# First mixer reworked: transposed input, norm after the projections, decay sums spread by transfers, memory projections a unit later

## The chip, the cores and the metric

The kernel runs on one core of one Trainium2 chip. The metric is the device time of one execution in microseconds (us); of several runs the median is given. The engines are named as in the profile: PE is TensorE's matmul, PEld its weight load, DVE is VectorE, ACT is ScalarE, POOL is GpSimd, SP is SyncE, whose queue issues every large transfer of this kernel.

## What is computed

A decoder trunk of two layers over 256 tokens of width 1024, in float32. Layer 0 mixes with a Mamba-2 scan (SSD), layer 1 with windowed attention; each also attends to 256 memory tokens and ends in a mixture of 32 experts. The parts of the reference that the change touches:

```
proj = rms_norm(h, norm_w) @ in_w
z, xbc, dt, q_mem = jnp.split(proj, [...], axis=-1)
xbc = jax.nn.silu(causal_depthwise_conv(xbc, conv_w, conv_b))
dt = jax.nn.softplus(dt + dt_bias)
# scan over 2 chunks of 128 tokens, 4 groups of 6 heads:
acum = jnp.cumsum(ac, axis=1)
seg = acum[:, :, None] - acum[:, None, :]
decay = jnp.exp(jnp.where(causal, seg, -jnp.inf))
y_diag = jnp.einsum('blsgr,bsgrp->blgrp', cb[..., None] * decay, xc)
...
kv = (rms_norm(mem, norm_w) @ w_kv)       # memory attention, in each layer
```

## The kernel before, in words

The program is a row of stages: the first mixer (`mixer_a`, 0 to about 289 us), the experts of layer 0 (to about 760 us), the second mixer, the experts of layer 1, the final norm.

**First mixer.** PE, DVE and ACT walk the same list, `order`, of small units of work such as `("conv", 3)` or `("yd", 0)`; each engine does its part of a unit and waits on semaphores for the others. A unit owns a PSUM bank, handed out in list order by `Units`. The list goes: `xT`, four units that turn the normed input by PE transposes (L336), behind the norm, which ACT and DVE do first on rows (L415 to L425); `dt`, 16 small matmuls whose stationary operand is the turned input (L893); 20 `conv` units, the projection of 128 channels each as 8 matmuls of 128x256 (L397), of which DVE makes the convolution (L1034, L1036) and ACT the silu; six `z` units (matmuls of 128x512) with transposes between; and then the scan. The scan has eight steps (2 chunks by 4 groups). Step i has `("cb", i)`; two `A` units, in which PE spreads the running sum of one head over all partitions, by a matmul of the broadcast `adt` column with the triangle (L930, 6 matmuls in a step); the decay arithmetic on DVE and ACT in four buffers `E` (L1060, L807, L988); and `("yd", i)`, the product with them (L956), one step later. A list `between` puts projections for the memory attention into each step. Then come `outm` (L365) and `out` (L380), the output projection, and the router.

**Transfers.** Weights pass through 18 slots of 1 MB (`own`, `late`, `extra`). SP issues the loads in the order of use, each when the slot's last user has finished, so one wait holds back everything behind it. The layer's first 18 expert loads follow the mixer's.

**Experts.** Twelve units a layer (`units_of`): eight wide ones with two experts of 64 tokens (12 loads of 1 MB each), four narrow ones with four experts of 32 tokens (24 loads each). A unit: gate and up projections (L1407), gather for the next unit (L1382), down projection (L1416), scatter (L1399). At the head of the units in `SIDE`, in layer 0 alone, PE also makes one of the two memory projections for layer 1 (`side`, L1438 and L1441); their weights are two 1 MB loads each, put in front of that unit's. Before the router's counting matmuls, PE does three idle matmuls (L513).

Of the kernel before, what the change touches and what calls it, by code (L numbers as in the profile page):

```python
# [28 lines left out]
P = 128  # L29
# [18 lines left out]
NEG = -1e30  # L48
GRAN = 2048
# [9 lines left out]
FIELDS = [("ident", P), ("tri", P), ("ones", P), ("iota", SEQ), ("band_prev", P), ("band_cur", P),  # L59
          ("index8", EG), ("cos", NT * 16), ("sin", NT * 16),  # L60
          ("a_norm", KD), ("mem_norm0", KD), ("mem_norm1", KD), ("kv_norm", KD), ("b_norm", KD),
          ("ffn_norm0", KD), ("ffn_norm1", KD), ("ffn_rows0", KD), ("ffn_rows1", KD), ("conv_w", NCONV * 4), ("conv_b", NCONV), ("gnorm", INNER // P),
          ("dt_bias", SSD_HEADS), ("a_log", SSD_HEADS), ("d_skip", SSD_HEADS), ("sinks", Q_HEADS),
          ("route_b0", NG + NE), ("route_b1", NG + NE), ("route_w0", KD * (NG + NE)), ("route_w1", KD * (NG + NE)),
          ("dt_w", KD * SSD_HEADS)]
# [20 lines left out]
SIDE = [NU - 4, NU - 2]  # L86
# [355 lines left out]
class Router:  # L442
# [51 lines left out]
    def pe(self, pe, key):  # L494
# [123 lines left out]
def mixer_a(c):  # L618
# [5 lines left out]
             "out_tile mem1_dve " + Router.SEMS)  # L624
    s = c.sems("mixer", names)
    ld_small = c.sem("ld_small")
    ld_x, ld_mem = ([c.sem(f"ld_{n}{t}") for t in range(NT)] for n in ("x", "mem"))
    with ctx:
# [13 lines left out]
        cbm = [sb(f"cbm{i}", P) for i in range(2)]  # L642
        xw = [acc[:, i * GW:(i + 1) * GW] for i in range(2)]
        sq = xw

# [13 lines left out]
        order = [("xT", i) for i in range(4)] + [("dt", 0)]  # L659
        order += [("conv", j) for j in range(NCONV)]  # L660
        order += [("z", 0), ("xtok", 0), ("xtok", 1), ("xtok", 2), ("bt", 0), ("ac", 0), ("z", 1), ("xtok", 3), ("xtok", 4), ("xtok", 5)]
# [14 lines left out]

        def freed(kind, i):
# [4 lines left out]
            return {"xT": (s["xT_ev"], 2 * i + 2), "dt": (s["dt_dve"], 1), "conv": (s["conv_dve"], 4 * i + 4),  # L682
                    "xtok": (s["xtok_ev"], i + 1), "bt": (s["bt_ev"], 1), "ac": (s["ac_dve"], 2), "z": (s["z_ev"], i + 1),
                    "q": (s["q_ev"], i + 1), "memT": (s["mem1_dve"], i + 1), "mk": (s["mk_ev"], i + 1),
                    "mv": (s["mv_ev"], i + 1), "cb": (s["cb_dve"], i + 1), "A": (s["seg_dve"], 3 * i + 3),
# [5 lines left out]
        U = Units(c, order, freed, holds)  # L691
# [18 lines left out]
        x_norm = Norm(c, c.h, 0, s["x_act"], s["x_dve"])  # L710
# [7 lines left out]
        def _(sp):  # L718
            for t in range(NT):
                sp.dma_start(cut(c.h, t=NT)[:, t, :], g["x"][0, t * P:(t + 1) * P, :]).then_inc(ld_x[t], 16)  # L720
            sp.dma_start(c.small[:, :], g["small"]).then_inc(ld_small, 16)
            for n in range(2):
                c.load_mixer_tile(sp, n)
# [1257 lines left out]
```

## Time and profile before

| | |
|---|---|
| median of 3 runs | 1394.44 us (1393.88 to 1397.04) |
| the profiled execution, its own time | 1395.1 us |
| its span, first to last instruction | 1393.2 us |
| PE busy | 1243.3 us, 89% |
| DVE, ACT busy | 280.8 us, 205.9 us |
| DMA, mean over the span | 329 GB/s; 427 GB/s where it is full |
| mean granted clock | 0.956 |

The span in 40 slices gives each about 34.8 us: the first mixer is slices 1 to 8, the experts of layer 0 slices 9 to 22. A busy PE in such a table is not a PE at its peak. Each matmul in float32 shows as two records in the trace, so "x16" is eight matmuls.

### The profile page before, as it was taken

What the parts mean: (1) busy time and instruction counts of PE and PEld (TensorE: products, weight loads), DVE (VectorE), ACT (ScalarE), POOL (GpSimd) and SP (SyncE); (2) the same over time, 40 slices, a digit from 0 to 9 for tenths busy, and PEclk for the clock granted to TensorE, in tenths of its full rate; (3) what the DMA queues carried; (4) which work ended last, traced back from release to release, by engine and by line L of the source; (5) the groups of instructions that cost most, each with busy time, mean ns of one, the idle gap of its engine ahead of it and who ended that gap; (6) DMA issues with size and microseconds to landing.
All of it is one profiled execution on the core that took longest, in us unless ns stands there. A gap on an engine that the chain in (4) does not pass through costs nothing. (4 is left out here: it accounts for less than half of the span.)

```text
span 1393.2 us, 15227 instructions
## 1 busy us (share of the span) xinstructions
PE 1243.3 (89%) x6130; PEld 627.0 (45%) x6130; DVE 280.8 (20%) x679; ACT 205.9 (15%) x490; POOL 34.0 (2%) x42
## 2 busy tenths in 40 slices
PE   6999999989999999769686998999999999757685
PEld 6875876454444445313232566454444443322221
DVE  3542453041111110100002156031111111100001
ACT  3124233120000000000002246130000000000001
POOL 0001210000000000000000011000000000000000
PEclk9999999999999999879899999999999999887897
DMA  9543307559999997999999722439999999999994
GB/s 378 188 159 121 122 0 287 226 220 425 425 425 420 426 425 318 427 425 426 427 426 388 299 103 91 182 139 417 423 419 427 425 427 427 425 427 426 427 427 177
DMA packets 78282, 458.78 MB, mean 329 GB/s; under 512 B 7040, under 2 KB 7040, under 8 KB 28928
## 3 DMA queue, kind: packets, MB, share of 16 engines
q1 hardware_dynamic: 78208, 457.75, 79.7%
q8 instruction: 52, 0.85, 0.2%
q14 instruction: 22, 0.18, 0.0%
HBM read 456.67 MB, written 1.05 MB: 329 GB/s over the span
## 5 line engine op out<-in xcount | busy, mean ns | idle before, releaser
L1407 PE MATMUL bank<-own,e_xg 128*64 128x512 f32 (+1 forms) x1272 | 273.9, 642 | 38.8 <-DMA late<-in_w_up 9.6
L1407 PE MATMUL bank<-late,e_xg 128*32 128x512 f32 (+1 forms) x648 | 167.8, 656 | 15.2 <-DMA late<-in_w_gate 7.3
L1407 PEld LDWEIGHTS bank<-own,e_xg 128*64 128x64 f32 (+1 forms) x1272 | 79.4, 130 | 203.4 <-issue 203.3
L1416 PE MATMUL bank<-own,e_turned 128*64 128x512 f32 (+1 forms) x592 | 129.2, 675 | 33.2 <-DMA own<-in_w_down 19.9
L1299 DVE TENSOR_TENSOR e_hid<-e_silu,bank 128x512 f32<-128x512 f32 x24 | 25.6, 1068 | 507.9 <-ACT e_silu L1350 507.9
L1416 PE MATMUL bank<-late,e_turned 128*64 128x512 f32 (+1 forms) x392 | 91.1, 680 | 16.8 <-DMA late<-in_w_down 7.6
L1382 PEld LDWEIGHTS bank<-e_pick,xs 128*128 128x128 f32 x768 | 93.4, 199 | 22.4 <-issue 18.7
L1382 PE MATMUL bank<-e_pick,xs 128*128 128x128 f32 x768 | 99.8, 286 | 3.5 <-DVE e_pick L1241 3.5
L1350 ACT ACTIVATE e_silu<-bank 128x512 f32<-128x512 f32 x24 | 14.3, 598 | 545.3 <-PE bank L1407 545.3
L1407 PEld LDWEIGHTS bank<-late,e_xg 128*32 128x32 f32 (+1 forms) x648 | 46.6, 132 | 96.9 <-issue 96.8
L1399 PE MATMUL bank<-e_y,e_gates_T 128*128 128x512 f32 x192 | 86.5, 593 | 1.4 <-ACT e_gates_T L1358 1.4
L397 PE MATMUL bank<-a_xnT,own 128*128 128x256 f32 x384 | 86.0, 387 | 0.0
L1416 PEld LDWEIGHTS bank<-own,e_turned 128*64 128x64 f32 (+1 forms) x592 | 36.6, 135 | 106.6 <-issue 96.0
L397 PEld LDWEIGHTS bank<-a_xnT,own 128*128 128x128 f32 x384 | 74.4, 195 | 10.4
L1304 DVE COPY e_y<-bank 128x512 f32<-128x512 f32 x24 | 16.6, 692 | 246.6 <-PE bank L1416 246.6
L1407 PE MATMUL bank<-extra,e_xg 128*64 128x512 f32 (+1 forms) x128 | 61.9, 629 | 0.0
L1416 PEld LDWEIGHTS bank<-late,e_turned 128*64 128x64 f32 (+1 forms) x392 | 24.9, 135 | 61.2 <-issue 56.2
L1399 PEld LDWEIGHTS bank<-e_y,e_gates_T 128*128 128x128 f32 x192 | 34.6, 190 | 36.3 <-issue 34.4
L1356 ACT ACTIVATE e_y<-bank 128x512 f32<-128x512 f32 x24 | 14.3, 597 | 233.9 <-PE bank L1416 233.9
L1252 DVE TENSOR_TENSOR e_xg<-bank,small 128x512 f32<-128x512 f32 x48 | 33.2, 692 | 48.4 <-PE bank L1382 48.4
L397 PE MATMUL bank<-own,a_xnT 128*128 128x512 f32 x96 | 42.1, 593 | 0.0
L380 PE MATMUL bank<-own,a_xbcT 128*128 128x512 f32 x96 | 41.8, 593 | 0.0
(341 smaller groups left out, 1120.6 us busy)
## 6 DMA issues: line engine op xcount, KB each, us to landing
own<-in_w_gate SPq DMA_DIRECT2D x83, 1024.0 KB, 12.5
own<-in_w_up SPq DMA_DIRECT2D x76, 1024.0 KB, 10.6
own<-in_w_down SPq DMA_DIRECT2D x74, 1024.0 KB, 12.4
late<-in_w_down SPq DMA_DIRECT2D x49, 1024.0 KB, 11.3
late<-in_w_up SPq DMA_DIRECT2D x41, 1024.0 KB, 11.4
late<-in_w_gate SPq DMA_DIRECT2D x40, 1024.0 KB, 12.7
own<-in_a_in_w SPq DMA_DIRECT2D x18, 1024.0 KB, 12.4
extra<-in_w_up SPq DMA_DIRECT2D x11, 1024.0 KB, 12.0
```

The costliest lines, as they stand in the source:

```text
L380: ins = pe.matmul(U.bank(("out", 2 * t + half))[:, :], src(t, 4 * (m - n) + j), c.rows_at(m, j)[:, 512 * half:512 * half + 512], start=Fal ...
L397: ins = pe.matmul(out, lhsT(k), rhs(k), start=(k == 0), stop=(k == n - 1))
L1252: dve.tensor_tensor(cut(self.xg[:, 512 * half:512 * half + 512], k=4), cut(bank, k=4), spread_last(c.f(f"ffn_norm{layer}", 4 * half, 4 * h ...
L1299: dve.tensor_tensor(self.hid[:, :].rearrange("q (h j p) -> q h p j", h=2, j=2), by_half(self.silu), by_half(self.b_up), ALU.mult).then_inc ...
L1304: dve.tensor_copy(self.y[1][:, :], self.b_down[1][:, :]).then_inc(s["y_ready"], 1)
L1350: act.activation(self.silu[:, :], self.b_gate[:, :], ACT.Silu).then_inc(s["silu_done"], 1)
L1356: act.activation(self.y[0][:, :], self.b_down[0][:, :], ACT.Copy).then_inc(s["y_ready"], 1)
L1382: ins = pe.matmul(bank[:, k * P:(k + 1) * P], xs[:, t, 4 * half + k, :], cut(self.pick, t=NT)[:, t, :], start=(t == 0), stop=(t == NT - 1))
L1399: ins = pe.matmul(self.sums[2 * t + out][:, :], self.gates_T[:, t * P:(t + 1) * P], self.y[out][:, :], start=first, stop=last, skip_group_ ...
L1407: ins = pe.matmul(bank[q * T:(q + 1) * T, :], self.xg[:, at:at + T], cut(tile(q), k=4)[:, k, :], start=(half == 0 and k == 0), stop=(half ...
L1416: ins = pe.matmul(self.b_down[out][q * T:(q + 1) * T, :], self.turned[:, at:at + T], cut(tile(q), j=2)[:, j, 512 * out:512 * out + 512], s ...
```

## The change

- The host passes `x` transposed as well (`xT`). The mixer's first loads are now the fields of `small` that the beginning needs (564 of 2176 columns), then parts of `xT` and of the first weight tile in turn; the rest of `small`, `mem` and `x` follow later.
- ACT scales `xT` by the norm's weight (`xTw`). The first four `conv` units project `xTw`, which is not normed yet. DVE squares `xT`; a unit `ss` sums the squares by a matmul with ones, which leaves the sum on every partition; from it DVE and ACT make `rb`, one factor per token. The four units are multiplied by `rb` when they leave PSUM; for everything later DVE makes `xnT` from `xTw` and `rb`. The `xT` units and the row norm are gone.
- `dt`: the weights are the stationary operand (32 columns, unit `dtp`, 8 matmuls in four column groups), and two small matmuls turn and sum the result (`dt`).
- The `A` matmuls are gone. One matmul (`acT`) makes all running sums as 48 rows; SP stores them to DRAM and loads each step's rows, broadcast to all partitions, into the buffers `E`: two loads of 192 KB in a step, issued when the `yd` two steps earlier has finished. They stand in SP's queue ahead of the loads of the output weights.
- `SIDE` is `[NU - 3, NU - 2]` instead of `[NU - 4, NU - 2]`: the first memory projection moves from the ninth unit to the tenth.
- One more idle matmul before the counting (four), and two at the head of each expert stage, before the first gather.

The core of the diff (`...` marks what is left out):

```diff
-SIDE = [NU - 4, NU - 2]
+SIDE = [NU - 3, NU - 2]
...
-            for _ in range(3):
+            for _ in range(4):
                 pe.matmul(out[:, :], c.f("ident"), c.small[:, 0:512], start=True, stop=True)
...
-        order = [("xT", i) for i in range(4)] + [("dt", 0)]
-        order += [("conv", j) for j in range(NCONV)]
+        order = [("conv", 0), ("conv", 1), ("ss", 0), ("conv", 2), ("conv", 3), ("dtp", 0)]
+        order += [("conv", j) for j in range(4, 10)] + [("dt", 0)] + [("conv", j) for j in range(10, NCONV)]
...
-        U = Units(c, order, freed, holds)
+        pe_order = [key for key in order if key[0] != "A"]
+        U = Units(c, pe_order, freed, holds)
...
+            def load_decays(st):
+                for i in (2 * st, 2 * st + 1):
+                    ch, gr = steps[st]
+                    row = SSD_HEADS * ch + HG * gr + 3 * (i % 2)
+                    rows = acum_rows[row:row + 3, :].rearrange("(o r) l -> o (r l)", o=1)
+                    sp.dma_start(E[i % 4][:, :], rows.broadcast_to([P, GW])).then_inc(e_loaded[i % 4], 16)
...
+            for n in range(5, TILES_A):
+                if n == TILES_A - 4:
+                    sp.wait_ge(s["acT_ev"], 1)
+                    sp.dma_start(acum_rows, acT).then_inc(s["acum_stored"], 16)
+                    sp.wait_ge(s["acum_stored"], 16)
+                    for st in range(len(steps)):
+                        sp.wait_ge(c.units_done, (U.at["yd", st - 2] if st >= 2 else U.at["memT", 3]) + 1)
+                        load_decays(st)
...
+            for k in range(KD):
+                act.wait_ge(ld_xT[min(k // 2, 2)], 16)
+                act.activation(cut(xTw, k=KD)[:, k, :], cut(xT, k=KD)[:, k, :], ACT.Copy, scale=c.f("a_norm", k, k + 1)).then_inc(s["xw_ev"], 1)
...
+                elif kind == "dtp":
+                    pe.wait_ge(s["xn_dve"], 2)
+                    for k in range(KD):
+                        q = DT_ROWS * (k % 4)
+                        ins = pe.matmul(out[q:q + DT_ROWS, 0:SEQ], cut(c.f("dt_w"), k=KD)[:, k, :], cut(xnT, k=KD)[:, k, :],
+                                        start=(k < 4), stop=(k >= 4))
...
+                U.wait_done(dve, ("ss", 0))
+                dve.tensor_scalar(rb[:, :], U.bank(("ss", 0))[:, 0:SEQ], 1.0 / D, EPS, ALU.mult, ALU.add).then_inc(s["rb_dve"], 1)
+                dve.wait_ge(s["rb_act"], 1)
+                dve.reciprocal(rb[:, :], rb[:, :]).then_inc(s["rb_dve"], 1)
...
+                    dve.tensor_tensor(cut(xnT, k=KD)[:, k, :], cut(xTw[:, :], k=KD)[:, k, :], spread_mid(rb[:, :], 4), ALU.mult).then_inc(s["xn_dve"], 1)
...
+                    if i < 4:
+                        step(dve.tensor_tensor(raw[i], bank[:, 0:SEQ], rb[:, :], ALU.mult))
+                        bank = raw[i]
...
-                    U.wait_done(dve, key)
-                    if i >= 4:
-                        dve.wait_ge(c.units_done, U.at["yd", (i - 4) // 2] + 1)
+                    dve.wait_ge(e_loaded[i % 4], 16 * (i // 4 + 1))
...
+                keep_busy(2)
                 pe.wait_ge(s["pick"], 1)
                 gather(0, s["gathered"])
```

What the change does to the order of instructions stands in three places. The first is PE's program from its beginning to the fifth `conv` unit (`xs` holds the turned input of before and `xTw` now, `a_xnT` the normed one, `small` the constants). Before:

```order
L336 MATMUL bank<-small,xs 128x128 [waits mixer_x_dve,ld_small]
L336 MATMUL bank<-small,xs 128x128 x15
L893 MATMUL bank<-small,a_xnT 128x24 [waits mixer_xT_ev]
L893 MATMUL bank<-small,a_xnT 128x24 x15
L397 MATMUL bank<-a_xnT,own 128x256 [waits w_loaded1,w_loaded0]
```

Now:

```order
L940 MATMUL bank<-xs,own 128x256 [waits mixer_xw_ev,ld_w0,ld_first]
L940 MATMUL bank<-xs,own 128x256 [waits mixer_xw_ev]
L940 MATMUL bank<-xs,own 128x256 [waits w_loaded0,mixer_xw_ev]
L940 MATMUL bank<-xs,own 128x256 x12
L946 MATMUL bank<-xs,own 128x256 [waits mixer_xw_ev,w_loaded1] x4
L946 MATMUL bank<-xs,own 128x256 x4
L401 MATMUL bank<-extra,small 128x256 [waits mixer_sq_dve]
L401 MATMUL bank<-extra,small 128x256 x7
L946 MATMUL bank<-xs,own 128x256 x8
L960 MATMUL bank<-a_xnT,small 32x256 [waits mixer_xn_dve]
L960 MATMUL bank<-a_xnT,small 32x256 x7
L401 MATMUL bank<-a_xnT,own 128x256 [waits ld_small,w_loaded3,w_loaded2]
```

The projections (L940, L946) now begin the program, the sum of squares stands between them, and the normed input is first waited for at L960. The second place is SP's queue between the last weights of the projections and the first expert (`a_qT` holds the running sums as rows, `xs` is `E`). Before, `own<-in_a_out_w` follows `own<-in_mem_w_kv` at once; now:

```order
L255 DMA own<-in_mem_w_kv 128x4x512 [waits units_done] x4
L763 DMA acum_rows<-a_qT 48x128 [waits mixer_acT_ev]
L741 DMA xs<-acum_rows 128x384 [waits units_done,mixer_acum_stored]
L741 DMA xs<-acum_rows 128x384
L741 DMA xs<-acum_rows 128x384 [waits units_done]
...
L255 DMA own<-in_a_out_w 128x2x1024 [waits units_done] x8
```

One store and 16 loads in eight pairs stand ahead of the output weights, each pair behind a wait on PE. The third is PE in the experts of layer 0, where the first memory projection (`memT`) stands. Before, between a wide unit's scatter and the first narrow unit:

```order
L1382 MATMUL bank<-e_pick,xs 128x128 x8
L1399 MATMUL bank<-e_y,e_gates_T 128x512 x4
L1438 MATMUL bank<-memT,late 128x256 x32
L1407 MATMUL bank<-late,e_xg 32x512 x2
```

Now, one unit later, between two narrow ones:

```order
L1507 MATMUL bank<-own,e_turned 32x512 x2
L1484 MATMUL bank<-small,e_gated 128x128 x2
L1473 MATMUL bank<-e_pick,xs 128x128 x8
L1490 MATMUL bank<-e_y,e_gates_T 128x512 x4
L1529 MATMUL bank<-memT,own 128x256 x32
L1498 MATMUL bank<-own,e_xg 32x512 x19
```

The 32 matmuls are the same; what stands ahead of them is a unit of four experts instead of one of two.

## Rows read from the trace of the kernel before

**Rows 1.** Page, part 2: the span in 40 slices

```profile
PE   6999999989999999769686998999999999757685
...
GB/s 378 188 159 121 122 0 287 226 220 425 425 425 420 426 425 318 427 425 426 427 426 388 299 103 91 182 139 417 423 419 427 425 427 427 425 427 426 427 427 177
```

**Rows 2.** Timeline of 0 to 100 us; start us, us, engine, line, op, out<-in, xcount

```profile
10.62 3.65 PE L336 MATMUL bank<-small,xs 128*128 128x128 f32 x16 [10.62 <-DVE xs L425]
...
15.19 7.03 PE L893 MATMUL bank<-small,a_xnT 128*128 128x24 f32 x32 [0.93 <-ACT a_xnT L774]
...
22.05 71.66 PE L397 MATMUL bank<-a_xnT,own 128*128 128x256 f32 x320
...
28.21 0.54 DVE L1034 TENSOR_SCALAR a_acc<-bank,small 128x256 f32<-128x256 f32 x1 [1.21 <-PE bank L397]
...
93.55 7.03 PE L397 MATMUL bank<-own,a_xnT 128*128 128x512 f32 x16
```

**Rows 3.** Windows of 5 us at the start: busy us of each engine, clock, DMA

```profile
0.00:5.00 5.00, 0.00 (x0) 0.00 (x0) 0.00 (x0) 1.88 (x2) 0.20 (x4) 1.00 0.64 219
5.00:10.00 5.00, 0.00 (x0) 0.00 (x0) 2.69 (x6) 3.28 (x7) 0.51 (x1) 1.00 0.97 379
```

**Rows 4.** Page of the DMA issues: xcount, KB each, median us to landing

```profile
out<-h SPq DMA_DIRECT2D x2, 512.0 KB, 2.6
memT<-in_final_norm_w SPq DMA_DIRECT2D x1, 512.0 KB, 3.6
```

**Rows 5.** Groups by shape, VectorE, 0 to 300 us; busy us, mean ns of one

```profile
L1060 DVE TENSOR_SCALAR xs<-bank,a_acum 128x128 f32<-128x128 f32 x48 | 13.6, 340 | 0.8 <-PE bank L930 0.8
L988 DVE TENSOR_TENSOR xs<-xs,a_cbm 128x384 f32<-128x384 f32 x16 | 10.9, 684 | 0.1
...
L1080 DVE TENSOR_TENSOR a_xbcT<-a_xbcT,a_smc 128x512 f32<-128x512 f32 x4 | 2.8, 692 | 0.1
...
L423 DVE RECIPROCAL norm_r<-norm_r 128x1 f32<-128x1 f32 x4 | 0.7, 164 | 3.2 <-ACT norm_r L417 3.2
...
L1017 DVE RECIPROCAL a_dt<-a_dt 128x48 f32<-128x48 f32 x1 | 0.5, 453 | 0.0
```

**Rows 6.** Timeline of one scan step, TensorE

```profile
149.01 1.50 PE L930 MATMUL bank<-small,a_dt 128*128 128x128 f32 x12
...
150.35 3.62 PE L397 MATMUL bank<-a_xnT,own 128*128 128x256 f32 x16
...
154.45 1.45 PE L956 MATMUL bank<-late,xs 128*128 128x64 f32 x12
```

**Rows 7.** Timeline of PE: product of the sixth scan step; start of the output projection

```profile
194.04 1.45 PE L956 MATMUL bank<-late,xs 128*128 128x64 f32 x12
...
217.80 3.60 PE L365 MATMUL bank<-own,a_qT 128*128 128x512 f32 x8
```

**Rows 8.** Windows around and after the first memory projection of the expert stage

```profile
528.00:550.00 22.00, 22.00 (x120) 14.89 (x122) 1.32 (x3) 1.19 (x2) 0.00 (x0) 1.00 0.63 257
550.00:755.00 205.00, 157.50 (x940) 58.58 (x932) 12.99 (x19) 9.64 (x22) 0.00 (x0) 0.88 1.01 425
```

**Rows 9.** Timeline and waits of the transfer queue at that projection

```profile
531.11 13.98 PE L1438 MATMUL bank<-memT,late 128*128 128x256 f32 x64
...
SPq L251 <- PE bank L1438: 18.5, 1, 18.5
```

**Rows 10.** Windows of 1 us and timeline at the expert stage's first gather

```profile
288.00:289.00 1.00, 0.26 (x3) 0.15 (x2) 0.90 (x6) 0.00 (x0) 0.00 (x0) 1.00 0.00 0
...
292.00:293.00 1.00, 1.00 (x7) 1.00 (x7) 0.00 (x0) 0.00 (x0) 0.00 (x0) 0.50 0.03 8
...
286.96 0.41 PE L516 MATMUL bank<-a_acc,small 128*128 128x32 f32 x2 [1.12 <-DVE a_acc L593]
...
290.03 5.27 PE L1382 MATMUL bank<-e_pick,xs 128*128 128x128 f32 x32 [1.77 <-DVE e_pick L1241]
```

**Rows 11.** Timeline, matmuls of 32 rows of experts' tokens

```profile
702.47 3.64 PE L1407 MATMUL bank<-own,e_xg 128*32 128x512 f32 x32
```

More of the change, by code:

```diff
@@ L741, in _ @@
         def _(act):
-            for t in range(NT):
-                act.wait_ge(ld_x[t], 16)
-                x_norm.act(act, t)
+            act.wait_ge(ld_first, 16)
+            act.activation(c.norm_r[:, 6:7], c.f("ones", 0, 1), ACT.Sqrt)
+            for k in range(KD):
+                act.wait_ge(ld_xT[min(k // 2, 2)], 16)
+                act.activation(cut(xTw, k=KD)[:, k, :], cut(xT, k=KD)[:, k, :], ACT.Copy, scale=c.f("a_norm", k, k + 1)).then_inc(s["xw_ev"], 1)
+            act.wait_ge(s["rb_dve"], 1)
+            act.activation(rb[:, :], rb[:, :], ACT.Sqrt).then_inc(s["rb_act"], 1)
             for key in order:
@@ L830, in _ @@
                 if key == ("z", 0):
[L831 removed]
+                    act.wait_ge(c.units_done, U.at["conv", 3] + 1)
                     for t in range(NT):
@@ L871, in _ @@
         def _(pe):
-            for key in order:
+            pe.wait_ge(ld_first, 16)
+            for key in pe_order:
                 kind, i = key
@@ L879, in _ @@
                     U.wait_free(pe, key)
-                if kind == "xT":
+                if kind == "conv" and i < 4:
                     if i == 0:
-                        pe.wait_ge(ld_small, 16)
-                        pe.wait_ge(s["x_dve"], 6)
-                    norm_T_units(c, pe, out, i)
+                        pe.wait_ge(ld_w0, 16)
+                    for j in range(4) if i == 0 else ():
+                        for k in range(4):
+                            if j == 0:
+                                pe.wait_ge(s["xw_ev"], k + 1)
+                            if j == 0 and k == 2:
+                                c.wait_job(pe, ("mixer", 0, 0))
+                            pe.matmul(U.bank(("conv", j))[:, 0:256], c.cols_at(0, k)[:, P * j:P * j + P], cut(xTw, k=KD)[:, k, :],
+                                      start=(k == 0), stop=False)
+                    for k in range(4, KD):
+                        if i == 0:
+                            c.wait_job(pe, ("mixer", 0, 1))
+                            pe.wait_ge(s["xw_ev"], k + 1)
+                        ins = pe.matmul(out[:, 0:256], c.cols_at(0, k)[:, P * i:P * i + P], cut(xTw, k=KD)[:, k, :], start=False, stop=(k == KD - 1))
+                    ins.then_inc(c.units_done, 1)
+                elif kind == "ss":
+                    pe.wait_ge(s["sq_dve"], 2)
+                    project(c, pe, out[:, 0:256], lambda k: c.f("ones"), lambda k: cut(squares, k=KD)[:, k, :])
                 elif kind == "memT":
@@ L921, in _ @@
                     pe.matmul(out[:, 48:72], c.f("ones"), cut(adt, t=NT)[:, 0, :], start=True, stop=True).then_inc(c.units_done, 1)
+                elif kind == "acT":
+                    pe.matmul(out[0:NT * SSD_HEADS, 0:P], adt[:, :], c.f("tri"), start=True, stop=True).then_inc(c.units_done, 1)
                 elif kind == "cb":
@@ L925, in _ @@
                               start=True, stop=True).then_inc(c.units_done, 1)
-                elif kind == "A":
-                    ch, gr = steps[i // 2]
-                    for hh in range(3):
-                        hd = HG * gr + 3 * (i % 2) + hh
-                        ins = pe.matmul(out[:, hh * P:(hh + 1) * P], cut(adt, t=NT)[:, ch, hd:hd + 1].broadcast_to([P, P]),
-                                        c.f("tri"), start=True, stop=True)
-                    ins.then_inc(c.units_done, 1)
                 elif kind == "sc":
@@ L1006, in _ @@
                     continue
-                bank = U.bank(key)
+                bank = U.bank(key) if kind != "A" else None
                 if kind == "dt":
```

120 lines of the change are left out of this document (81 added, 39 removed).

## The prediction

> **What bounds the kernel now.** I began with the page's 40 slices [rows 1]. Its GB/s line shows two regimes. In the expert slices it reads about 427: there the end is set by when the next weights can be fetched. In the first eight slices it is low while PE reads 9 throughout: the first mixer is bound by PE's program, and whatever shortens that starts the experts' transfers, and so everything behind them, earlier by the same amount. One expert slice, the sixteenth, has 318 GB/s with PE full. So three stretches can give time: the mixer's head, its scan, and that hole.
>
> **The head.** The timeline [rows 2] shows PE silent until 10.62, behind the row norm on DVE (L425). Then transposes, `dt` for 7.03 us, the first projection from 22.05 and the first z unit at 93.55. DVE reads the first projection at 28.21, so it was done at about 28.0 and took 5.95; the other 19 took until 93.55, which is 3.45 each, full pace. The first had half pace, although PE had been at light work since 10.62.
>
> Now: PE needs the first constants, two of eight parts of `xT` and a quarter of a weight tile, 0.29 + 0.26 + 0.52 = 1.07 MB. The windows give 219 GB/s over the first 5 us, 1.1 MB [rows 3]; with the landing and one ACT scaling I take 5.6. Work up to the first z unit at full pace: 20 projections, 69.0; the sum of squares, the size of one, 3.45; `dtp`, eight matmuls of 256 columns on 32 rows, where 16 of 512 columns took 3.6 [rows 11], so 0.9; two small ones, 0.3. Together 73.6. To this come three losses. Pace: like the first projection before, the new first ones will run at half; I take half pace to about 12 us, which loses 2.7 (bounds: 2.5, what the first projection lost, and 6). Data: the third part of `xT` and of the weights is 1.86 MB into the queue, at about 7 us, 1.0 (0 to 2.5). And the norm: between `ss` and `dtp` lie DVE's read (0.55), ACT's root (0.4), a reciprocal of 256 columns, for which 1 and 48 columns at 0.164 and 0.453 give 1.7 along the line, and two products of 1024 columns, where 512 take 0.692 and part of that is fixed, some 1.2 each [rows 5]; with 0.5 for hand-overs 5.6 us. PE has two half projections, 3.45, to cover it: a wait of 2.2 (1.5 to 3.5). The first z unit then comes at 5.6 + 73.6 + 2.7 + 1.0 + 2.2 = 85.1 instead of 93.55: **8.4 saved**, bounds 4 and 10. DVE is late with four longer evictions (2.6 each) behind the norm, but gains 1.4 on every 3.45 later, and eight banks cover it: nothing.
>
> **The scan.** The six `A` matmuls of a step hold PE from 149.01 to 150.35 [rows 6], 1.34, and PE has no gap there. Eight steps: **10.7 saved**; the one `acT` matmul costs 0.15. In its place each pair of loads starts when a `yd` is finished. DVE takes the first of them before it finishes the factors of the step before, and the next `yd` waits for those. PE's cover is shortest in the steps with one projection between: from 150.35 to 154.45, 4.1, plus the short product, 4.35. Against that stand a hand-over of 0.2, the landing, DVE's three subtractions and one product, 3 x 0.34 + 0.68 = 1.7 [rows 5]; nothing else is in the queue, because SP holds the output weights back. Landing is not in the trace for 192 KB. From below: 512 KB out took 2.6, less 0.75 for the bytes, 1.85; from above: 512 KB of the one broadcast, beside expert weights, 3.6 [rows 4]. I take 2.9, nearer the broadcast, which it resembles: 0.45 late in each of two short steps, **1.0 lost** in all (0 to 4); the other steps cover 6 to 8 us. The 8 MB of output weights, held back to the last pair, now start when the sixth step's product ends, at what was 195.4 us, and need some 20 us; the first tile, in place 7 us after that, is wanted at 217.80 [rows 7] less the 1.3 of the last step, 14 us later, and the others follow faster than PE uses them. Nothing; were the last pair 14 us later, this would be the next wait.
>
> **The memory projection.** From 528 to 550 the transfers average 257 GB/s instead of 427, although PE is busy all the time [rows 8]. PE does the first memory projection there, 13.98 us from 531.11, and SP waits 18.5 us for it [rows 9], for it frees no expert's slot meanwhile. Missing: 22 x (427 - 257)/427 = 8.8 us. After 550 the rate is 425 while PE has 47 us of gaps, so in the narrow units the transfers set the end and PE has room. One unit later the 13.98 us fall into such room: a narrow unit is 24 MB, 59 us of transfer, and SP is 18 loads (44 us) ahead. **8.5 saved** (0 to 8.8).
>
> **Idle matmuls.** The fourth before counting fits in the 1.12 us that PE waits there [rows 10]. The two before the gather do not fit: PE sat idle only 1.77 us, most of it before the stage opens. The granted clock was 1.00 at 288 us and 0.50 at 292 (same rows), that is 2.4 and then 1.2 GHz, and the gather's 32 records took 5.2 us where 3.8 is full pace. If the clock stays up, a gather 1.1 later but 1.4 shorter gains 0.3; if it falls anyway, the two take twice as long and the gather starts 2.5 late. Two stages, **1.0 lost** together (-0.6 to 5).
>
> **A rule beside this.** In the row, 1.77 us without work behind light work was followed by the lower clock. The Trainium skill, "TensorE: Matmul & The Clock Gate", section "What's actually happening", says the clock follows how busy the array has recently been. By that rule the new wait of 2.2 us in the head can drop the clock as well, which by the gather's row would cost 1.4 more: 1370.4 instead of 1369.0. I leave it out of the sum, for dense matmuls stand on both sides there.
>
> **Sum.** -8.4 - 10.7 + 0.15 + 1.0 - 8.5 + 1.0 = -25.4. The profiled execution took 1395.1, 1.9 over its span, which gives 1369.7; the median of the runs shown lies 0.7 under that execution, so **1369.0**.
>
> **Rivals.**
> - The hole stays, because any memory projection in the narrow units holds SP as long. For it: the second one stands right behind now. Against: the second already stood in a narrow unit, and the mean after 550 holds no such hole. Then 1377.5. Chance 0.10.
> - The loads land late, in 5 us: 2.5 lost in each short step, none in the long, 4 more than in the sum: 1373. Chance 0.08.
> - The head does not pay: the wait for the norm keeps PE at 1.2 GHz until it is over. Then 23 us of dense work from 5.6 on run at half pace, 11.5 lost instead of 2.7: 1377.8. For it: half pace lasted from 10.62 to past 22.05 before. Against: that work was light, and the first dense projection ended it. Chance 0.08.
> - Slower: the pairs land as a 1 MB load in a filled queue does, in 12 us. Waits of 9.5 in two short steps, 5.5 in three long ones, 7.7 in the last come to 43: 1369 + 42 = 1411. It decides from a landing of about 8.8 us, where 6 x 8.8 - 27 eats the 25.4. Against: SP issues nothing between pairs, so the queue is empty. Chance 0.03.
> - The changed parts do not act at all: the two kernels' instruction orders show that they do. The rest, 0.01, goes to slower mishaps.
>
> **How the numbers follow.** The forecast has the remaining 0.70. Its own bounds are 1364 (head 10, no late loads, clock kept) to 1376. Most of the first and third rivals lie within 1378; so 1362 to 1379 leaves out under two in ten. A measurement of this kernel can tell about 0.2%, 2.8 us, from no change. Faster by more: all but the fourth rival, 0.96. Within it: 0.01. Slower: 0.03.
>
> **What would show it.** PE's first matmul at 5.6 and first z unit near 85; no L930, and each short scan step about 5.9 instead of 7.0; landing of the pairs under 3 us; 427 GB/s across the place of the hole, with PE gaps further on smaller by 14; first expert matmul near 278 instead of about 295. The forecast is wrong if PE waits for DVE in every scan step, if the transfers pause near the tenth unit, or if projections up to 30 us take 6.9.

## The result, and the profile after

| | before | after |
|---|---|---|
| median | 1394.18 us (1392.96 to 1397.04, 8 runs) | 1386.69 us (1383.7 to 1391.32, 8 runs) |
| profiled execution, span | 1395.1, 1393.2 us | 1383.7, 1381.9 us |
| first z unit | 93.55 | 86.47 |
| output projection starts | 217.80 | 203.75 |
| first expert matmul, layer 0 | 295.22 | 280.93 |
| second mixer's first transposes | 761.45 | 745.38 |
| first expert matmul, layer 1 | 935.53 | 920.33 |
| last scatter | 1378.57 | 1367.19 |

The ratio is 0.9948, 95% interval 0.9929 to 0.9967: faster by 7.5 us, where 25.4 were forecast. The time lies 7.7 us above the range of the forecast: the sign is right, the size is not.

The rows of the table come from PE's timelines, and their differences say where the time is. At the first expert matmul of layer 0 the changed kernel is 14.3 us ahead. The expert stage of layer 0 should add 8.5 and adds 1.8 (466.23 us before, 464.45 after). The experts of layer 1, which the change does not touch, take 3.8 us longer (443.04, 446.86). So the largest loss is in the transfer-bound stages. The page's 40 slices of after show it (compare [rows 1]; the eleventh to the fourteenth slice are full in both):

```profile
PE   6999999999999998877778998999999999657685
...
GB/s 347 294 122 54 52 286 340 183 304 421 420 422 421 421 422 414 423 416 421 421 421 355 231 61 92 212 196 422 420 422 420 421 421 421 421 421 422 421 421 180
```

The hole of 318 in the sixteenth slice is gone, but a full slice now reads 421 where it read 427. That is 1.4% less in every stretch that the transfers bind. Windows over the place of the hole and over the narrow units (busy us of each engine, clock, DMA share, GB/s):

```profile
515.00:537.00 22.00, 21.53 (x185) 7.85 (x183) 1.90 (x3) 1.26 (x3) 0.00 (x0) 1.00 1.02 421
...
550.00:650.00 100.00, 80.53 (x450) 37.62 (x448) 5.34 (x9) 4.54 (x10) 0.00 (x0) 0.91 1.02 420
```

The DMA share is 1.02: the engines are not waiting, each packet takes longer. [Rows 8] had 425 GB/s at a share of 1.01 there.

The head, in the timeline of after (start, us, engine, line, op, out<-in, count, idle before and its releaser; compare [rows 2]):

```profile
3.63 0.20 ACT L784 ACTIVATE norm_r<-small 128x1 f32<-128x1 f32 x1 [1.60 <-DMA small<-in_small]
5.62 0.91 ACT L787 ACTIVATE xs<-memT,small 128x256 f32<-128x256 f32 x2 [1.78 <-DMA memT<-in_xT]
...
8.20 2.04 PE L940 MATMUL bank<-xs,own 128*128 128x256 f32 x4 [8.20 <-DMA own<-in_a_in_w]
...
10.66 6.87 PE L940 MATMUL bank<-xs,own 128*128 128x256 f32 x28 [0.42 <-DMA own<-in_a_in_w]
...
20.82 3.62 PE L401 MATMUL bank<-extra,small 128*128 128x256 f32 x16
...
24.55 0.42 DVE L1061 TENSOR_SCALAR a_cbm<-bank 128x256 f32<-128x256 f32 x1 [11.48 <-PE bank L401]
...
25.46 1.75 DVE L1063 RECIPROCAL a_cbm<-a_cbm 128x256 f32<-128x256 f32 x1 [0.48 <-ACT a_cbm L789]
27.25 2.36 DVE L1068 TENSOR_TENSOR a_xnT<-xs,a_cbm 128x1024 f32<-128x1024 f32 x2
...
29.66 1.07 PE L960 MATMUL bank<-a_xnT,small 128*32 128x256 f32 x16 [1.77 <-DVE a_xnT L1068]
```

The norm chain is as forecast: the reciprocal of 256 columns 1.75 (1.7 said), a product of 1024 columns 1.18 (1.2), the wait 1.77 (2.2). PE however starts at 8.20 instead of 5.6. ACT's scaling ran from 5.62 and was in time; the quarter weight tile was late. The first 5 us moved little (window; columns as above):

```profile
0.00:5.00 5.00, 0.00 (x0) 0.00 (x0) 0.00 (x0) 1.49 (x2) 0.20 (x4) 1.00 0.51 136
5.00:10.00 5.00, 1.80 (x4) 1.17 (x4) 0.74 (x1) 1.73 (x4) 0.00 (x0) 1.00 1.00 335
```

136 GB/s where [rows 3] had 219. In the scan, two places of the timeline of after and the waits of PE in the first mixer (line waited for, us in total, times, longest):

```profile
144.21 1.52 PE L1025 MATMUL bank<-late,xs 128*128 128x64 f32 x12 [0.23 <-issue]
...
180.17 0.79 SPq L741 DMA_DIRECT2D xs<-acum_rows  x2
...
181.01 7.17 SPq L255 DMA_DIRECT2D own<-in_a_out_w  x7
...
185.49 0.68 DVE L1151 TENSOR_SCALAR xs<-xs,a_acum 128x128 f32<-128x128 f32 x3 [1.02 <-DMA xs<-acum_rows]
...
187.13 1.10 PE L348 MATMUL bank<-late,a_qT 128*128 128x256 f32 x4 [2.40 <-ACT late L851]
```

```profile
PE bank L940 <- DMA own<-in_a_in_w: 8.6, 2, 8.2
PE bank L348 <- ACT late L851: 2.4, 1, 2.4
PE bank L960 <- DVE a_xnT L1068: 1.8, 1, 1.8
PE bank L1516 <- PEq L635: 1.3, 1, 1.3
```

A scan step with one projection is 6.1 us (138.15 to 144.21), 5.9 said. The one real wait of PE in the scan is the last: SP issues the last pair at 180.17 and the output weights right behind it, the pair lands 4.9 us after its issue, ACT is held up behind DVE, and PE waits 2.4 us for ACT.

### The profile page after: what moved, and what is told of

It is laid out like the page before. It is cut to its first block and busy times, and to the rows that moved or that the text cites. A ratio compares the mean times of both kernels' runs of the same rounds, so it can differ in the third digit from the quotient of the medians.

```text
span 1381.9 us, 15072 instructions
## 1 busy us (share of the span) xinstructions
PE 1227.8 (89%) x6036; PEld 608.3 (44%) x6036; DVE 281.3 (20%) x683; ACT 203.9 (15%) x488; POOL 32.7 (2%) x42
## 3 DMA queue, kind: packets, MB, share of 16 engines
HBM read 460.91 MB, written 1.07 MB: 334 GB/s over the span
## 5 line engine op out<-in xcount | busy, mean ns | idle before, releaser
L1498 PE MATMUL bank<-own,e_xg 128*64 128x512 f32 (+1 forms) x1272 | 267.4, 635 | 36.2 <-DMA own<-in_w_gate 10.1
L1498 PE MATMUL bank<-late,e_xg 128*32 128x512 f32 (+1 forms) x648 | 162.9, 648 | 16.2 <-DMA own<-in_w_up 7.7
L1498 PEld LDWEIGHTS bank<-own,e_xg 128*64 128x64 f32 (+1 forms) x1272 | 78.3, 130 | 199.0 <-issue 198.9
L1507 PE MATMUL bank<-late,e_turned 128*32 128x512 f32 (+1 forms) x408 | 94.9, 671 | 25.2 <-DMA own<-in_w_down 11.3
L1473 PEld LDWEIGHTS bank<-e_pick,xs 128*128 128x128 f32 x768 | 89.6, 192 | 19.6 <-issue 19.6
L1473 PE MATMUL bank<-e_pick,xs 128*128 128x128 f32 x768 | 95.5, 278 | 0.0
L1441 ACT ACTIVATE e_silu<-bank 128x512 f32<-128x512 f32 x24 | 14.3, 597 | 539.5 <-PE bank L1498 539.5
L401 PE MATMUL bank<-a_xnT,own 128*128 128x256 f32 x320 | 70.1, 380 | 0.0
L401 PEld LDWEIGHTS bank<-a_xnT,own 128*128 128x128 f32 x320 | 60.4, 190 | 8.4 <-issue 0.4
L1507 PEld LDWEIGHTS bank<-late,e_turned 128*32 128x32 f32 (+1 forms) x408 | 25.8, 134 | 73.1 <-issue 66.2
L1447 ACT ACTIVATE e_y<-bank 128x512 f32<-128x512 f32 x24 | 14.3, 597 | 241.6 <-PE bank L1507 241.6
L1516 PE MATMUL bank<-small 128*128 128x512 f32 x88 | 41.9, 622 | 2.6 <-PEq L1624 1.3
## 6 DMA issues: line engine op xcount, KB each, us to landing
own<-in_a_in_w SPq DMA_DIRECT2D x17, 1024.0 KB, 14.3
```

Source lines behind the costliest of these rows:

```text
L401: ins = pe.matmul(out, lhsT(k), rhs(k), start=(k == 0), stop=(k == n - 1))
L1441: act.activation(self.silu[:, :], self.b_gate[:, :], ACT.Silu).then_inc(s["silu_done"], 1)
L1447: act.activation(self.y[0][:, :], self.b_down[0][:, :], ACT.Copy).then_inc(s["y_ready"], 1)
L1473: ins = pe.matmul(bank[:, k * P:(k + 1) * P], xs[:, t, 4 * half + k, :], cut(self.pick, t=NT)[:, t, :], start=(t == 0), stop=(t == NT - 1))
L1498: ins = pe.matmul(bank[q * T:(q + 1) * T, :], self.xg[:, at:at + T], cut(tile(q), k=4)[:, k, :], start=(half == 0 and k == 0), stop=(half ...
L1507: ins = pe.matmul(self.b_down[out][q * T:(q + 1) * T, :], self.turned[:, at:at + T], cut(tile(q), j=2)[:, j, 512 * out:512 * out + 512], s ...
```

## The experiments

**Theory S** (place): the constants in `small` grew from 2080 to 2176 columns, 384 bytes in each partition, and all weight slots, which are allocated behind it, moved by that. The rival theories: R, the new tensors in device memory (`xT`, `acum_rows`) moved the weights there; M, the moved memory projection or the loads of the scan changed the traffic; N, nothing but the chip's spread. (The first expectations call R theory H, and M and N together C.) The trace's 49180 weight packets of 8 KB measure the rate without the rest of the program: in before, 309 ns each from the 5th to the 95th percentile, mean 312.3; in after 309, 309, 312, 316, 321 ns at the 5th, 25th, 50th, 75th, 95th, mean 315.7.

### The slots moved in the kernel before

```diff
+        self.pad = self.sb("pad", 96)
         self.own = self.sb("own", OWN * GRAN)
```

> The kernel before with 96 unused columns (384 bytes a partition) ahead of the weight slots, which puts them where the changed kernel has them. Theory S, the slots' place in SBUF: an 8 KB weight packet goes from 309 ns to about 312 to 316, the full rate from 427 to 421 GB/s, and with some 900 us bound by transfers the time rises by 8 to 11 us, to about 1404. Theories H (place in HBM) and C (the changed kernel's own traffic or chance): no change, 1394.

Measured: 1401.59 us (1400.38 to 1405.3, 4 runs) beside 1394.5, ratio 1.0057 (1.0035 to 1.0079). One unused buffer makes the kernel 7.1 us slower, a little less than the 8 to 11 expected but outside the spread, so theory N falls. The packets' mean is 315.6 ns, and the page's slices read:

```profile
GB/s 365 226 131 120 121 0 322 195 250 421 421 422 420 422 416 345 422 416 421 421 421 379 291 88 91 180 153 422 422 421 421 421 421 421 421 421 422 421 421 186
```

### The slots moved on in the kernel after

```diff
+        self.pad = self.sb("pad", 32)
         self.own = self.sb("own", OWN * GRAN)
```

> The changed kernel with 32 unused columns ahead of the weight slots, so that these stand 512 bytes, and not 384, behind their place in the kernel before. Theory S, if what counts is the place within 512 bytes: packets of 309 ns and 427 GB/s again, and 8 to 13 us less than the changed kernel, 1374 to 1378. Theories H and C: no change, 1387.

Measured: 1379.53 us (1374.21 to 1381.58, 4 runs), ratio to before 0.9895 (0.9877 to 0.9913); 7.2 us less than after, again a little under the 8 to 13 expected. Packets 309 ns throughout, mean 312.1, and:

```profile
GB/s 360 285 123 55 47 240 378 188 255 425 421 423 426 427 426 421 426 424 427 427 427 370 259 62 93 186 203 423 426 423 426 426 423 426 426 427 427 426 427 186
```

The experts of layer 0 take 458.69 us instead of 464.45, those of layer 1 441.96 instead of 446.86: 10.7 us between these two profiles. The profile of this version is of its fastest run; the six traces at full rate that also have the moved projection took 458.7 to 460.5 and 441.6 to 443.0, so that 9.6 is the mean.

### Device memory

```diff
+    acum_rows = c.nc.dram_tensor("acum_rows", (NT * SSD_HEADS, P), F32).ap()
...
+    arrays["xT"] = np.ascontiguousarray(np.asarray(inputs["x"])[0].T).reshape(P, KD * SEQ)
```

> The kernel before with the transposed input and the scratch tensor in device memory, both unused: its tensors in device memory are those of the changed kernel. Theory H: 421 GB/s and about 1404. Theories S and C: 427 GB/s and 1394.

Measured: 1395.42 us (10 runs), ratio 1.0007 (0.9996 to 1.0018), packets 312.4 ns. Theory R falls.

### The memory projection back in its old unit, in the kernel after

```diff
-SIDE = [NU - 3, NU - 2]
+SIDE = [NU - 4, NU - 2]
```

> The changed kernel with the first memory projection back in the ninth unit. If the hole in the transfers was worth its length, the pause near the ninth unit returns (under 150 GB/s for some 5 us) and the time rises by 8.5 us, to about 1395. If the transfers would have made up for it later, no change from 1387.

Measured: 1395.14 us (1390.86 to 1397.3, 10 runs), ratio 0.9997 (0.9984 to 1.001). The move of one unit is worth 8.45 us by the medians, and 8.5 was the term. The traces give less to the stage itself: the experts of layer 0 take 469.11 us here and 464.45 in after, 4.7 apart, and the other 4.7 between the two spans stand in stages that this edit does not touch (the first expert matmul is at 284.08 instead of 280.93). At full rate it is 6.8: 466.2 to 466.7 us in four traces with the projection in its old unit, 458.7 to 460.5 in six with it moved. The hole is back (344 GB/s in the sixteenth slice), and SP waits 18.5 us for the projection as in [rows 9]:

```profile
SPq L255 <- PE bank L1529: 18.5, 1, 18.5
```

Full slices stay at 421 GB/s and packets at 315.7 ns, and the version with the 32 columns has the moved projection and the scan's loads at 427, so theory M falls too. With the projection back, all other parts together gain about what the slots cost: 1395.14 is before's time.

### The running sums by matmuls again

From here on all versions of after have the 32 unused columns. This one undoes the scan's part alone (store, loads and their waits out, `A` units back in PE's list):

```diff
-        pe_order = [key for key in order if key[0] != "A"]
+        pe_order = order
...
+                elif kind == "A":
+                    ch, gr = steps[i // 2]
+                    for hh in range(3):
+                        hd = HG * gr + 3 * (i % 2) + hh
+                        ins = pe.matmul(out[:, hh * P:(hh + 1) * P], cut(adt, t=NT)[:, ch, hd:hd + 1].broadcast_to([P, P]),
```

> The changed kernel with the slots put right (the 32 unused columns of the second experiment), and with the running sums spread by the matmuls of the kernel before instead of the store and the loads. If the transfers are worth what the traces show in the scan (5.3 to 7 us between the first z unit and the output projection), this takes 5 to 7 us more than 1379.5, about 1385.5. If DVE bounds the scan as it is, and the transfers bring nothing, no change.

Measured: 1386.5 us (1378.22 to 1388.65, 6 runs), ratio 0.9928 (0.9906 to 0.995). Against 1379.53 the transfers save 7.0 us by the medians, though the two intervals just overlap. By the timelines, first z unit to output projection takes 124.26 us here and 124.25 or 124.26 in all six versions of before. With the loads it takes 117.28 in after, but 118.94 in the version with the 32 columns, and 118.90, 118.97 and 117.54 in three more: 5.3 to 7.0 saved, 5.9 in the mean, where 9.55 were forecast. Windows over that stretch in after and in the version with the 32 columns, and one us of the latter:

```profile
86.47:203.75 117.28, 114.51 (x477) 75.95 (x476) 47.84 (x125) 43.15 (x96) 17.90 (x20) 1.00 0.34 121
```

```profile
87.88:206.82 118.94, 116.18 (x477) 77.10 (x476) 48.21 (x125) 43.12 (x96) 17.88 (x20) 0.99 0.34 119
189.00:190.00 1.00, 1.00 (x3) 0.79 (x3) 0.00 (x0) 0.00 (x0) 0.00 (x0) 0.50 1.02 422
```

The work is the same, but PE is busy 1.67 us longer. Behind the 2.4 us that PE waits for ACT (to 188.53 in this version) the granted clock fell to 0.50, half speed, from 189 to 192. So it did behind that wait in three of the five traces that have it; in the two where the wait is 1.2, and in the seven traces without the loads, it did not. That fits the wait as the cause; it is not proven by so few.

### The new idle matmuls out

```diff
-            for _ in range(4):
+            for _ in range(3):
...
-                keep_busy(2)
                 pe.wait_ge(s["pick"], 1)
```

> The changed kernel with the slots put right and without the new idle matmuls (three before the counting, none before the gather). My prediction had them cost 1.0 in all; the traces say that they gain 0.2 to 1.1. If they gain, this takes 0.5 to 2 us more than 1379.5 and the gather's 32 records take over 5 us again; if they cost, up to 1 us less.

Measured: 1379.01 us (4 runs), ratio 0.9889 (0.9875 to 0.9904): 0.5 us less than with them, within the spread. After, and below it this version, at the first gather of layer 0:

```profile
275.47 1.95 PE L1516 MATMUL bank<-small 128*128 128x512 f32 x4 [1.28 <-PEq L635]
277.26 3.73 PE L1473 MATMUL bank<-e_pick,xs 128*128 128x128 f32 x32
```

```profile
278.83 6.22 PE L1474 MATMUL bank<-e_pick,xs 128*128 128x128 f32 x32 [1.76 <-DVE e_pick L1333]
```

With them the gather starts later (3.5 us after the last counting matmul's start, against 2.15), but takes 3.73 us instead of 6.22. That is not the whole of it. In the version with the last pair first (the next experiment), the idle matmuls are there too and are themselves slow:

```profile
277.99 3.27 PE L1519 MATMUL bank<-small 128*128 128x512 f32 x4 [1.28 <-PEq L636]
281.06 4.13 PE L1476 MATMUL bank<-e_pick,xs 128*128 128x128 f32 x32
```

The fair measure is from the last counting matmul's start to the first expert matmul, and the traces have it for both layers. With the idle matmuls it is 7.12 to 8.81 us in twelve stage heads, 8.09 in the mean; without them 7.29 to 8.87 in sixteen, 8.20 in the mean. They shorten the gather every time (3.73 to 4.49 us, against 5.21 to 6.79), and take as much themselves. Neither the forecast's loss of 1.0 nor a gain can be told from nothing.

### The last pair before the output weights

```diff
                         load_decays(st)
+                    for i in range(2):
+                        sp.wait_ge(e_loaded[2 + i], 16 * 4)
```

> The changed kernel with the slots put right, and SP waits until the last pair of running sums has landed before it issues the output weights. Theory: the 2.4 us that PE waits in the eighth scan step come from the weights issued 0.5 us behind that pair, which let its second load land after 4.9 us instead of 3.1. Then the wait falls below 1 us and the time by 1.5 to 2, to about 1377.8. If the wait comes from the order of ACT's work alone, no change.

Measured: 1376.9 us (1375.72 to 1382.08, 4 runs), ratio 0.9871 (0.9857 to 0.9885). The landing of the pairs, in after and then here:

```profile
DMA to landing us min/median/max: 2.9/3.2/4.9
```

```profile
DMA to landing us min/median/max: 2.9/3.2/3.4
```

```profile
PE bank L349 <- ACT late L854: 1.2, 1, 1.2
```

The last row is PE's wait at the same matmul, half of after's 2.4. So it was the output weights that made the last pair late. First z unit to output projection is 116.37 us. In the version that differs by this edit alone it is 118.94, 2.6 more: 1.2 of the wait, and 1.7 of the lower clock that stood behind it there and not here, less 0.3 elsewhere; after, without that drop, has 117.28. The median is 2.6 us under the version without the edit as well, but the intervals overlap.

### The queue held at the start

```diff
+            sp.wait_ge(ld_w0, 16)
             c.load_mixer_half(sp, 0, 1)
```

> The changed kernel with the slots put right, and SP waits for the first quarter of the first weight tile before it issues the rest of that tile and what follows. Theory: that quarter lands at 8.2 us, not at 5.6 as I took, because the loads issued behind it share the transfer engines. Then the first matmul starts at 6 to 6.8 us, and the time falls by 0.5 to 2 us (the second half of the tile must come in time). If the queue serves in order, PE still starts at 8.2 and the second half comes later: no change or 1 us more.

Measured: 1378.67 us (1371.14 to 1381.89, 6 runs), ratio 0.9876 (0.9854 to 0.9898). PE starts at 7.31, but the experiment before, with the head of after, started at 7.01 without this, and after itself at 8.20: the start spreads by more than the edit's effect. The first z unit is at 89.80, no earlier. The run does not tell whether the held queue helps.

### Which places cost

The kernel before with 32, with 64 unused columns (128, 256 bytes) ahead of the slots, and with 96 behind them (`self.pad` after `extra`).

> The kernel before with 32 unused columns (128 bytes a partition) ahead of the weight slots; nothing else. If any step away from the place of before costs, the mean 8 KB weight packet takes 315 to 316 ns as with 384 bytes, the full pace is 421 GB/s instead of 427, and the profiled time is 5 to 9 us above before's. If only some places cost, it stays at 309 ns in its whole middle, 427 GB/s, and a time within 3 us of before's. With before and the steps of 384 (slow) and 512 bytes (full pace) this maps which places cost.

> The kernel before with 64 unused columns (256 bytes a partition) ahead of the weight slots. If the cost goes by whether the place is a multiple of 512 bytes away from before's, this one is slow like 384 bytes (packets of 315 to 316 ns, 421 GB/s, 5 to 9 us above before). If it goes by a multiple of 256 or 128 bytes, it is at full pace (309 ns, 427 GB/s, within 3 us of before).

> The kernel before with the same 96 unused columns as the first padded run, but behind the weight slots, so that the slots stay where they were and only what is allocated behind them moves. If it is the slots' place that costs, this is before's time within 0.2 percent, with packets of 309 ns and 427 GB/s. If it is the memory taken up, or the place of the other buffers, it is 0.4 to 0.7 percent slower like the first padded run.

Measured. The byte at which `own` starts is a count of what the program allocates ahead of it and stands in no trace; what the runs vary is the move in the first column. The times are of three sittings, in which before took 1393.3 to 1394.5:

| slots moved by | `own` starts at byte (by count) | over a multiple of 256 (by count) | mean packet, ns | GB/s when full | time, us |
|---|---|---|---|---|---|
| 0 (before) | 42240 | 0 | 312.3 | 427 | 1393.28 |
| 0, 96 columns behind | 42240 | 0 | 312.3 | 427 | 1394.88, ratio 1.001 (1.0 to 1.002) |
| 128 bytes | 42368 | 128 | 315.5 | 421 | 1406.61 (one run) |
| 256 bytes | 42496 | 0 | 312.3 | 426 to 427 | 1392.62 (one run) |
| 384 bytes | 42624 | 128 | 315.6 | 421 | 1401.59 |
| 384 bytes (after) | 42624 | 128 | 315.7 | 421 | 1386.69 |
| 512 bytes (after with 32 columns) | 42752 | 0 | 312.1 | 427 | 1379.53 |

Windows over the same 100 us of the narrow units, moved by 128 bytes and then by 256:

```profile
550.00:650.00 100.00, 75.27 (x469) 29.07 (x462) 7.80 (x12) 4.85 (x11) 0.00 (x0) 0.88 1.02 420
```

```profile
550.00:650.00 100.00, 76.89 (x452) 30.09 (x445) 7.80 (x12) 4.85 (x11) 0.00 (x0) 0.86 1.01 426
```

Every version whose slots are moved by 0, 256 or 512 bytes has packets of 309 ns from the 5th to the 95th percentile, and every one moved by 128 or 384 has the slower ones: all fourteen kernels sort so without an exception. The Trainium skill, "DMA: Bandwidth & Descriptors", section "How a descriptor splits into AXI transactions", says that a transfer goes in transactions of 256 bytes that must start on a multiple of 256, so that one off it needs an extra one and fetches bytes that it does not use. By that rule an 8 KB packet that starts 128 bytes off has 33 transactions instead of 32, and 260 beats of 32 bytes instead of 256, an estimate of 1.6%; the traces show 1.1% (312.3 to 315.7) and agree in kind. The page speaks of reads; here it is the place written to that was moved, so the rule as the cause is an inference, while the period of 256 bytes is measured.

### The best version

After with 32 columns, without the new idle matmuls, and with the last pair ahead of the output weights.

> After with 32 unused columns ahead of the slots, without the new idle matmuls, and with SP holding the output weights until the last pair of running sums has landed. By the theory: slots at full pace (7 us of the change's shortfall), the last pair 1 to 1.5 us sooner, idle matmuls nothing or 0.5 us. Against the version with the columns alone (0.9895) a gain of 0 to 3 us: 1376 to 1379.5 us where before takes 1394, a ratio of 0.987 to 0.9895; the last pair lands within 3.6 us. If the two small edits do nothing at all, 0.9895 again.

Measured: 1374.03 us (1372.32 to 1376.6, 4 runs) beside 1393.28, ratio 0.9861 (0.9845 to 0.9878): 19.3 us faster than before, 12.7 faster than after, and 2 us under the lower end of what was expected. The last pair landed in 3.5 us, and PE's wait behind it is 1.2. The interval touches that of the version with the columns alone, so the two small edits together are likely, not certain, to help; taking the idle matmuls out has no share in it that can be told. The window from the first z unit to the output projection, beside after's 117.28 us above:

```profile
86.97:203.03 116.06, 114.48 (x477) 75.98 (x476) 47.60 (x125) 43.13 (x96) 17.89 (x20) 1.00 0.33 117
```

The 1.2 us of the pair are here in two windows at clock 1.00 and equal work (PE busy 114.51 and 114.48).

## Why the prediction was wrong, step by step

The sum was made against the profiled execution: 1369.7 forecast, 1383.7 measured, 14.0 apart. The columns in the middle are between the two profiled executions; the last takes the mean over all traces of this case in which the stage is unedited, of either kind.

| step | forecast | shown, two executions | short by | shown, means |
|---|---|---|---|---|
| head | -8.4 | -7.1 | 1.3 | -4.9 (6 and 7 traces) |
| scan, with `acT` and late loads | -9.55 | -7.0 | 2.6 | -5.9 (7 and 5) |
| stage head of layer 0, idle matmuls | +0.5 | -0.25 | -0.75 | -0.7 (6 and 6) |
| hole | -8.5 | -7.5 at full rate | 1.0 | -6.8 at full rate (4 and 6) |
| second mixer and its stage head | +0.5 | +0.9 | 0.4 | +2.0 (6 and 6) |
| layer 1 experts at full rate | 0 | -1.1 | -1.1 | -0.6 (4 and 6) |
| place of the slots, both expert stages | not in the sum | +10.7 | 10.7 | +9.6 |

The shortfalls come to 14.1. "Full rate" is the version with the 32 columns; in the last column, all versions at 427 GB/s. The last column adds up to -7.3, beside -7.5 by the medians, so it is the better account of the change; the one profiled execution of after flattered the head and the scan.

**What failed.** The step is one that the prediction does not have. It took the 427 GB/s of [rows 1] as a constant of the chip ("427 GB/s across the place of the hole"), and the diff's growth of `small`, 2080 to 2176 columns, as nothing. It is a property of the program: the constants are allocated ahead of the slots, and with 384 bytes more the slots left the places that run at full rate (by count, the multiples of 256). Two padded kernels (+7.1 and -7.2 us by medians) and the four places show it; no rival had it either. But it is not all. With the slots put right the kernel took 1379.53, still 10.5 above the forecast of 1369.0 and just past the range: by the medians the slots are 7.2 of the 17.7 missed, and most of the other 10.5 is in the head and in the scan, which by the means fell 3.5 and 3.6 short.

**The head**: mechanism right, sizes mixed. PE's start was mis-sized by 2.6 (8.20 for 5.6). The 1.07 MB were divided by the rate of two large loads; but several small loads, and behind them more in the same queue, gave 136 GB/s over the first 5 us, and the weight tile's quarter came 6.5 us after its issue. On the other side, PE needed 78.3 us from its start to the z unit where the terms come to 79.5: wait 0.4 less, data 0.6 less, pace 0.9 less, the rest 0.7 more. Half pace to about 12 us was right in after, but after was lucky: of the eight versions with the new head its first z unit is the earliest (86.47; the others 86.97 to 89.89). In the version with the 32 columns half pace lasted to 15 us, as the counts of PE's records in two windows show:

```profile
14.00:15.00 1.00, 1.00 (x4) 0.79 (x4) 0.00 (x0) 0.00 (x0) 0.00 (x0) 1.00 0.98 393
15.00:16.00 1.00, 1.00 (x7) 0.87 (x6) 0.00 (x0) 0.00 (x0) 0.00 (x0) 1.00 1.02 401
```

The clock column reads 1.00 in both. The traces hold no record of the clock before its first rise (11.8 us in after, 14.8 here), and that column takes its absence for full speed; only the count tells the pace there.

The rule of the clock that was weighed there, that the 2.2 us wait could drop it, did not come true in after: granted clock 1.00 on both sides of the 1.77 us. It did in two others of the eight, the one with the last pair first and the one with the held queue: behind the same 1.77 us wait the clock was 0.50 from 33 to 36 us, and from the `dtp` matmuls to the first z unit it took 58.5 us instead of 56.8, 1.7 lost where 1.4 had been named and left out of the sum. With the last pair first:

```profile
33.00:34.00 1.00, 1.00 (x4) 0.72 (x4) 0.93 (x3) 0.28 (x1) 0.00 (x0) 0.50 1.04 403
```

The third rival (half pace until the norm) did not come true: in after the 28 records from 10.66 took 6.87, where 6.05 is full pace, and in all eight the full pace was there before 16 us.

**The scan**: the 8 x 1.34 are there, and the landing of 2.9 was right for a queue that is empty (2.9 to 3.4 here). Late loads were priced at 1.0 and cost 3.6 in all. Of this the last pair is 2.4, and it fell with the sentence "SP issues nothing between pairs": nothing stands between pairs, but behind the last one 8 MB follow at once, and transfers issued behind a small load slow it (4.9 us). The prediction named the last pair only as what releases the output weights, not as what suffers from them. The remaining 1.2 of the 3.6 are small: 0.2 to 0.4 us a step in the rows, not resolved further. In three of five traces the lower clock behind the last pair's wait adds 1.7, a term that the sum does not have. The second rival (landing in 5 us) came true for the last pair alone; the one on the slower side (12 us) did not.

**The memory projection**: mechanism right, size a little high. 8.5 forecast, 8.45 by medians, but 6.8 in the traces at full rate and 4.7 at the slower one, so that the 8.45 is partly luck. The first rival (the hole stays) is out: 421 GB/s from 515 to 537.

**The idle matmuls**: 1.0 loss forecast; 0.5 loss by the medians, within their spread, and 0.1 us a stage gained by the traces' means, within theirs. They took about as much time as the gather gained by them.

**From profile to median.** The forecast took the median 0.7 under the profiled execution; it lies 3.0 over it in after. The traces place it in the mixers, where PE sets the time: against the means of the versions of after, this execution is 1.4 us early at the first z unit, 1.0 shorter in the scan and 1.5 in the second mixer. Windows over the second mixer with the stage head behind, in the version with the 32 columns, in after, and in the one with the last pair first:

```profile
742.70:915.64 172.94, 161.49 (x654) 97.28 (x654) 62.20 (x210) 65.01 (x184) 13.88 (x17) 1.00 0.45 173
```

```profile
745.38:920.33 174.95, 164.16 (x654) 99.15 (x654) 62.21 (x210) 65.39 (x184) 13.90 (x17) 0.98 0.45 171
```

```profile
745.26:923.61 178.35, 167.56 (x655) 100.41 (x655) 62.21 (x210) 65.40 (x184) 13.91 (x17) 0.96 0.43 168
```

The same stage takes 172.9, 175.0 or 178.4 us at a mean granted clock of 1.00, 0.98 or 0.96. The profiled execution of after was its fastest run (1383.7 of 1383.7 to 1391.3). Together, 14.0 and the 3.7 of this, are the 17.7 us by which 1386.7 missed 1369.0. After's runs also spread more than before's (7.6 us and 4.1 us). The drops behind its two new waits, 1.7 us each and only in some executions, are a likely part; before has neither wait, and its scan took 124.25 or 124.26 us in every trace. No run was made to test it.

## What to carry to other kernels

Where transfers set the time, look at where their buffers start: on this kernel a place off by 128 or 384 bytes cost 7 us, and any tensor allocated ahead can move them there, so align the weight buffers explicitly and compare the full-rate GB/s of two traces before anything else. A small load that something waits for needs the queue quiet behind it as well as ahead of it. And read a stage's gain from its own two ends in both traces, and in more than one trace of each, for one execution can flatter a stage by 1 to 3 us: here 14.3 us gained in the first mixer stood beside 10.7 lost in the expert stages, partly in code that nobody had changed.

## What the runs showed of the hardware

- A weight packet of 8 KB took 309 ns (mean 312.3) into slots at before's place or moved by 256 or 512 bytes, and 309 to 321 ns (mean 315.6) into slots moved by 128 or 384; the full rate went from 427 to 421 GB/s with the DMA share at 1.01 and 1.02. The shift of 256 bytes alone cost nothing (1392.62 us beside 1393.28).
- A broadcast load of 192 KB landed in 2.9 to 3.5 us in a quiet queue, and in 4.9 with 1 MB loads issued behind it.
- With two idle matmuls ahead of it a gather of 32 records took 3.73 to 4.49 us, without them 5.21 to 6.79; but the idle matmuls took 1.95 to 3.46 us themselves, and the two together came to the same (8.09 and 8.20 us in the mean from the last counting matmul to the first expert matmul).
- Behind a wait of PE of 1.77 us in dense matmuls the granted clock fell to 0.50 in two of eight traces, behind one of 2.40 us in three of five, behind one of 1.22 us in none of two; each drop cost 1.7 us.
- The first matmul, which waits for the same loads, began at 7.01 to 9.20 us in the eight versions with the new head, and full pace came at 11.8 to 15.7; the first z unit, at 86.47 to 89.89, spread by 3.4 us with it and with the drop behind the norm's wait.
